# Four layers of token mixing on one core: 64-row products in alternate halves, compression products in column quarters, and a new order of the first transfers

## The reference, cut to what matters

```python
# compression (even layer): 15 windows of 32 tokens, 2 groups, window flattened to 4096
blk = (t[:, cmp_gather] + pe[:, None, :]).transpose(0, 1, 3, 2, 4).reshape(B, n_cmp, G, 32 * 128)
hid = silu(einsum('bcgf,fh->bcgh', blk, w1))        # w1: 4096 x 256
out = einsum('bcgh,hd->bcgd', hid, w2)              # once for keys, once for values
# retention, chunks of 128: contraction over 64
scores = einsum('bhtd,bhsd->bhts', qc, kc) * intra
# HGRN: a decay for each of the 64 channels between any two tokens of a chunk
scores = einsum('bhtd,bhsd,bhtsd->bhts', qc, kc, pair)
# RWKV
log_w = -DECAY * sigmoid(w0 + tanh(wd) @ w_up); a = sigmoid(a0 + ad @ a_up)   # 64 rows each
state = state * exp(lw) - (state @ kk) (a * kk) + v k ;  y = state @ r
```

## Time and profile before

| | us |
|---|---|
| median of 3 runs | 3870.77 (3852.96 to 3872.96) |
| the profiled execution | 3863.83 |
| its span | 3862.4 |
| PE busy | 3780.9 (98%), 19948 records |
| PE weight loads | 3190.6 (83%) |
| DVE busy | 2243.5 (58%) |
| ACT busy | 1793.4 (46%) |
| POOL busy | 113.0 (3%) |
| moved by DMA | 628.34 MB, mean 163 GB/s |
| mean granted clock of PE | 0.991 of full speed |

### The profile page before, as it was taken

The page is one execution under the profiler, slowest core; times in us unless marked ns, Lnnn a source line. Parts: engine busy times, 40 slices in busy tenths (PEclk is TensorE's granted clock), DMA queues, the critical chain, the costliest instruction groups (busy, mean ns, idle before and its releaser), DMA issues.

```text
span 3862.4 us, 49187 instructions
## 1 busy us (share of the span) xinstructions
PE 3780.9 (98%) x19948; PEld 3190.6 (83%) x19948; DVE 2243.5 (58%) x3532; ACT 1793.4 (46%) x2517; POOL 113.0 (3%) x61
## 2 busy tenths in 40 slices
PE   8999999999999999989999999999999999999998
PEld 7886778787898998778888888888987778888887
DVE  5665666676565746674455444566656764445444
ACT  6454545456554425454444444554335454444443
POOL 0000000000010000000000000010000000000000
PEclk9999999999999989999999999999999999999999
DMA  7655546563554315456666655544224456666654
GB/s 237 187 164 148 147 147 176 159 191 119 172 166 138 109 27 170 136 158 188 189 190 188 201 194 193 178 141 147 69 81 150 161 162 190 190 191 186 203 194 169
DMA packets 341426, 628.34 MB, mean 163 GB/s; under 512 B 21088, under 2 KB 63024, under 8 KB 340432
## 3 DMA queue, kind: packets, MB, share of 16 engines
q1 hardware_dynamic: 331920, 611.53, 52.5%
q10 hardware_dynamic: 9280, 13.69, 1.0%
HBM read 623.04 MB, written 2.10 MB: 162 GB/s over the span
## 4 chain that ended last, share of the span: by engine, by line
PE 92%; DVE 4%; ACT 2%; issue 1%; DMA 1%; POOL 0%; ACTq 0%; SPq 0%; DVEq 0%
PE bank L635 77%; PE bank L763 1%; DVE weights_low L529 1%; PE bank L1338 1%; PE bank L1435 1%; PE bank L2545 1%; PE bank L2559 1%; PE bank L2151 1%; PE bank L2558 1%; ACT weights_high L516 1%; PE bank L614 1%; PE bank L1418 1%; PE bank L1341 0%; PE bank L2512 0%; PE bank L1317 0%
## 5 line engine op out<-in xcount | busy, mean ns | idle before, releaser
L529 DVE TENSOR_TENSOR weights_low<-weights,weights_high 128x1024 fp32r<-128x1024 f32 (+3 forms) x1176 | 1392.4, 1194 | 994.2 <-ACT weights_high L516 983.4
L516 ACT ACTIVATE weights_high<-weights 128x1024 fp32r<-128x1024 f32 (+3 forms) x1176 | 1205.1, 1029 | 1308.6 <-PE bank L635 1250.8
L635 PE MATMUL bank<-weights_high,x_high 128*128 128x512 f32 (+3 forms) x2816 | 1111.4, 395 | 8.8 <-DVE weights_low L529 2.9
L635 PE MATMUL bank<-weights_low,x_high 128*128 128x512 f32 (+3 forms) x2816 | 1082.7, 384 | 0.0
L635 PE MATMUL bank<-weights_high,x_low 128*128 128x512 f32 (+3 forms) x2816 | 1081.4, 384 | 0.0
L635 PEld LDWEIGHTS bank<-weights_high,x_high 128*128 128x128 f32 x2816 | 532.3, 189 | 121.7 <-issue 15.1
L635 PEld LDWEIGHTS bank<-weights_low,x_high 128*128 128x128 f32 x2816 | 531.8, 189 | 101.5
L635 PEld LDWEIGHTS bank<-weights_high,x_low 128*128 128x128 f32 x2816 | 533.2, 189 | 92.8
L635 PE MATMUL bank<-x_high,weights_high 128*128 128x256 f32 x960 | 279.5, 291 | 9.5 <-DVE arena L664 4.8
L635 PE MATMUL bank<-weights_high,y_high 128*128 128x512 f32 (+1 forms) x672 | 266.7, 397 | 8.9 <-DVE weights_low L529 5.9
L635 PE MATMUL bank<-weights_high,ff_high 128*128 128x512 f32 x704 | 274.0, 389 | 0.0
(11 more groups left out here) (384 smaller groups left out, 3597.7 us busy)
## 6 DMA issues: line engine op xcount, KB each, us to landing
weights<-in_w_in_dram SPq DMA_DIRECT2D x208, 512.0 KB, 3.6
weights<-in_w_ffn_gate_dram SPq DMA_DIRECT2D x176, 512.0 KB, 3.7
weights<-in_w_ffn_up_dram SPq DMA_DIRECT2D x176, 512.0 KB, 3.7
weights<-in_w_ffn_down_dram SPq DMA_DIRECT2D x176, 512.0 KB, 3.6
weights<-in_w_out_dram SPq DMA_DIRECT2D x128, 512.0 KB, 3.7
weights<-in_even_w_in_dram SPq DMA_DIRECT2D x88, 512.0 KB, 3.6
weights<-in_odd_w_in_dram SPq DMA_DIRECT2D x80, 512.0 KB, 3.7
weights<-in_mem_w_kv_dram SPq DMA_DIRECT2D x32, 512.0 KB, 4.4
```

The source lines that it names most:

```text
L516: self.high_mark[g] = self.high_split.count(act.ran(nc.scalar.activation(high, raw, ACT.Copy)), act.clock)
L529: self.low_mark[g] = self.low_split.count(dve.ran(nc.vector.tensor_tensor(low, raw, high.bitcast(F32), ALU.subtract)), dve.clock)
L635: ins = pe.ran(nc.tensor.matmul(out, l, r, start=(u + c + x + y == 0), stop=(u == blk.n - 1 and c == UNIT - 1 and y == 1)))
```

## The change

Four edits. (1) In `retention`, `hgrn` (both places) and `rwkv` (three places), the products of two heads on opposite halves are issued in turn, into two banks, behind one wait for both banks; what follows on DVE and ACT stays as it was, head by head. PE's price of a 64-row product is halved in the planner when the one before lay on the other half. (2) A compression unit's four matmuls go to four quarters of the array's columns, 32 weights each, and so to partitions 0 to 127 of the bank; each quarter adds up a fourth of the sum. The bank is evacuated by a plain copy, and the transposes become products with a folded identity that add the quarters; ACT then applies Silu to the 60 columns. The planner's price of these units is the old one. (3) SP issues memory rows and weights in turn, two pieces and one unit, and a piece of x behind each of the units 8 to 15. (4) `first_turns` turns all memory rows with the splits between and the squares behind, and turns x only when block mem0.v is done.

```diff
@@ -206,7 +208,10 @@
             n = max(2 * n, 240)
         else:
             n = n + 32 if one.ins[0].dtype == F32R else max(4 * n + 24, 536)
-        self.clock += n / 2400
+        rows = one.tile_position[0] if one.ins[0].ap[0][1] <= HD2 else None
+        beside = rows is not None and self.rows not in (None, rows)
+        self.rows = rows
+        self.clock += n / 2400 / (2 if beside else 1)
         return ins
 
     def did(self, ins):
...
             self.plan()
-            for g in range(AHEAD):
+            for g in range(RAW):
                 self.load(g)
-            self.load_x()
-            for g in range(AHEAD, RAW):
-                self.load(g)
+                if g < 3:
+                    self.load_mem(g + 1)
             self.later = self.load_rest()
             for k in range(7):
                 next(self.later)
...
@@ -502,6 +506,14 @@
             dst = self.raw[i][:, :, 0:blk.width]
         self.sp.clock += 1.7
         self.load_mark[g] = self.loaded[i].count(self.nc.sync.dma_start(dst, blk.src[u]), self.sp.clock + 2.2)
+        if X_FROM <= g < X_FROM + 4 * T:
+            self.load_x((g - X_FROM) // T, (g - X_FROM) % T)
+
+    def split_to(self, g):
+
+        while self.split_next <= g:
+            self.split(self.split_next)
+            self.split_next += 1
 
     def split(self, g):
 
...
+            ins = pe.ran(nc.tensor.matmul(bank[l * QUARTER:(l + 1) * QUARTER, 0:CMP_HID], blk.AT[:, k * R2:k * R2 + QUARTER], wv[:, l, :],
+                                   start=(u == 0), stop=(u == blk.n - 1)))
         self.used_mark[g] = self.unit_used.count(ins, pe.clock + DRAIN)
         return self.used_mark[g]
 
...
+            self.sp.clock += 0.8
+            self.mem_loaded[nb].count(self.nc.sync.dma_start(self.mem[:, t, cut], self.A["mem"][0, t * P:(t + 1) * P, cut]), self.sp.clock + 2.5)
+
+    def load_x(self, nb, t):
+
+        cut = slice(nb * TILE, (nb + 1) * TILE)
+        self.sp.clock += 0.8
+        self.x_loaded[nb].count(self.nc.sync.dma_start(self.x[:, t, cut], self.A["x"][0, t * P:(t + 1) * P, cut]), self.sp.clock + 2.5)
 
     def load_rest(self):
 
...
@@ -979,7 +994,7 @@
 
         def evac(n, b, mark):
             act.wait_ge(mark)
-            m = act.did(nc.scalar.activation(self.hid[j][0:R2, :], self.ps[b][0:R2, 0:CMP_HID], ACT.Silu))
+            m = act.did(nc.scalar.activation(self.hid[j], self.ps[b][:, 0:CMP_HID], ACT.Copy))
             self.bank_free[b] = [m]
             return m
         return evac
...
-        yield
-        for nb in range(2, 4):
+        for nb in range(4):
             yield from turns(nb, self.hT_mem, *mem, self.mem_loaded[nb])
-            square(nb - 1, self.mem, self.mem_loaded[nb - 1])
+            if nb < AHEAD:
+                self.split_to(nb)
             yield
-        square(3, self.mem, self.mem_loaded[3])
+        for nb in range(4):
+            square(nb, self.mem, self.mem_loaded[nb])
+            yield
         self.rms_of(self.squares, self.scales["mem"])
         yield
+        yield from self.need("mem0.v")
         for nb in range(4):
             for _ in turns(nb, self.hT_even, self.x_chunk, self.col["norm0"], self.x_loaded[nb]):
                 yield _
...
         yield from self.need("e.kv0")
         self.ready(["e.kv0"], pe)
+        width = CMP_LEN * R2
+        for j in range(2):
+            dve.did(nc.vector.memset(self.blkT[j][:, width:width + 2], 0.0))
+        folded = dve.did(nc.vector.tensor_reduce(fold, self.c("ident").rearrange("p (g r) -> p r g", g=4), AX.X, ALU.add))
         for j in range(2):
             yield [*self.bank_free[6]]
             pe.wait_ge(*self.bank_free[6])
...
+            pe.wait_ge(folded, *self.bank_free[4])
             for c in range(2):
-                ins = pe.ran(nc.tensor.transpose(self.ps[4][:, c * R2:(c + 1) * R2], self.hid[j][0:R2, c * P:(c + 1) * P], self.c("ident")[0:R2, 0:R2]))
-            dve.wait_ge(pe.did(ins))
-            m = dve.did(nc.vector.tensor_copy(hidT[:, 0:2 * R2], self.ps[4][:, 0:2 * R2]))
+                ins = pe.ran(nc.tensor.matmul(self.ps[4][:, c * R2:(c + 1) * R2], self.hid[j][:, c * P:(c + 1) * P], fold[:, 0:R2], start=True, stop=True))
+            act.wait_ge(pe.did(ins))
+            m = act.did(nc.scalar.activation(hidT[:, 0:2 * R2], self.ps[4][:, 0:2 * R2], ACT.Silu))
             self.bank_free[4] = [m]
             yield
             yield [m, *self.bank_free[5]]
...
+            if h < H2 and h % 2 == 0:
+                at = h // 2 * S
+                both = [*self.bank_free[4], *self.bank_free[5]]
+                yield both
+                pe.wait_ge(*both)
+                for lo, cols in ((0, S), (P, P)):
+                    for e in range(2):
+                        half = slice(e * HD2, (e + 1) * HD2)
+                        ins = pe.ran(nc.tensor.matmul(self.ps[4 + e][:, 2 * lo:2 * lo + cols], kT[half, at + lo:at + lo + P],
+                                                      qT[half, at + lo:at + S], start=True, stop=True))
+                        if lo:
+                            scored[h + e] = pe.did(ins)
             if h < H2:
-                c, half, b = h // 2, slice(h % 2 * HD2, (h % 2 + 1) * HD2), 4 + h % 2
-                at = c * S
-                yield [*self.bank_free[b]]
-                pe.wait_ge(*self.bank_free[b])
-                pe.ran(nc.tensor.matmul(self.ps[b][:, 0:S], kT[half, at:at + P], qT[half, at:at + S], start=True, stop=True))
-                dve.wait_ge(pe.did(pe.ran(nc.tensor.matmul(self.ps[b][:, S:S + P], kT[half, at + P:at + S], qT[half, at + P:at + S],
-                                                    start=True, stop=True))))
+                b = 4 + h % 2
+                dve.wait_ge(scored[h])
                 if h >= 4:
                     dve.wait_ge(*weighed[h - 4][1:])
                 dve.did(nc.vector.tensor_tensor(sT[h % 4][:, 0:S], self.ps[b][:, 0:S], decay[:, h * S:(h + 1) * S], ALU.mult))
...
-                yield self.bank_free[b]
-                pe.wait_ge(*self.bank_free[b])
+            for pair in range(2):
+                both = [*self.bank_free[4 + 2 * pair], *self.bank_free[5 + 2 * pair]]
+                yield both
+                pe.wait_ge(*both)
                 for i in range(4):
-                    c, h = heads[4 * (g // 2) + g % 2 + 2 * (i // 2)]
-                    t = i % 2
-                    ins = pe.ran(nc.tensor.matmul(self.ps[b][:, i * P:(i + 1) * P], k3[h, c, t * P:(t + 1) * P], q3[h, c, t * P:(t + 1) * P],
-                                           start=True, stop=True))
-                multiplied[lev, g] = pe.did(ins)
+                    for e in range(2):
+                        g, t = 2 * pair + e, i % 2
+                        c, h = heads[4 * pair + e + 2 * (i // 2)]
+                        ins = pe.ran(nc.tensor.matmul(self.ps[4 + g][:, i * P:(i + 1) * P], k3[h, c, t * P:(t + 1) * P],
+                                                      q3[h, c, t * P:(t + 1) * P], start=True, stop=True))
+                        if i == 3:
+                            multiplied[lev, g] = pe.did(ins)
 
         def merge(lev, mask):
 
...
+        pe.wait_ge(*both)
+        crossed = []
+        for i in range(4):
+            for g in range(2):
                 c, h = heads[g + 2 * i]
                 ins = pe.ran(nc.tensor.matmul(self.ps[6 + g][:, i * P:(i + 1) * P], d3[h, c, 0:P], d3[h, c, P:S], start=True, stop=True))
-            act.wait_ge(pe.did(ins))
+                if i == 3:
+                    crossed.append(pe.did(ins))
+        for g in range(2):
+            act.wait_ge(crossed[g])
             m = act.did(nc.scalar.activation(cross[:, g * 512:(g + 1) * 512], self.ps[6 + g][:, :], ACT.Copy))
             self.bank_free[6 + g] = [m]
         yield from self.need(nm + "hgi", nm + "hgg")
...
+            for x in range(2):
+                for half in range(2):
+                    rows, c = slice(half * HD2, (half + 1) * HD2), 2 * pair + x
+                    ins = pe.ran(nc.tensor.matmul(self.ps[4 + 2 * pair + half][:, x * S:(x + 1) * S], lora[rows, c * P:(c + 1) * P], wa[rows, :],
+                                                  start=True, stop=True))
+                    if x:
+                        raised.append(pe.did(ins))
+            for half, (out, bias) in enumerate(((lw, "rwkv_w0_2"), (a, "rwkv_a0_2"))):
+                b, i = 4 + 2 * pair + half, 2 * pair + half
+                act.wait_ge(raised[half])
+                for x in range(2):
+                    c = 2 * pair + x
...
-                    n = 4 * grp + i
-                    t, c, e = units[n]
-                    b = 4 + i
-                    yield [*self.bank_free[b]]
-                    pe.wait_ge(*self.bank_free[b])
-                    pe.ran(nc.tensor.matmul(self.ps[b][:, 0:S].rearrange("p (k s) -> p k s", k=2), tile(a, c, t)[head(e), :], kr(c, t, e), start=True, stop=True))
```

(54 more changed lines are left out.)

61 lines of the change are left out of this document (24 added, 37 removed).

## The result

The changed kernel takes 3847.34 us (median of 17 runs, 3830.57 to 3860.82), the kernel before 3867.63 (17 runs). The ratio is 0.9949, 95% interval 0.9936 to 0.9962: 20 us faster (15 to 25), where 48 were forecast. The time lies inside the range of 3796 to 3852, near its slow end. The profiled execution took 3851.68, its span 3850.4, at a mean granted clock of 0.982, against 3863.83 at 0.991 before.

The account below looks back on a forecast made before the run. TensorE, holding 92% of the span, was taken as the bound. Halves 35, compression 12.5 and first transfers 4 give 51.5 us off 3863.8: 3812; clock cost makes 3817, half the median's 6.9 excess 3820 us; range 3796 to 3852.

Parts of the forecast that it names:

- The planner puts stream ahead of it as before, so I price it at 0: Each pair's wait for two free banks: stream chunks cover it, cost 0, up to 1.4 us a pair where they don't.
- All of it lies in PE's queue beside the stream of line 635, which fills every wait: The 35 us from pairing 64-row products: a shorter product makes the stream's next chunk earlier.
- the compression rival: Compression returns in full, as the planner or slack hides the softmax: 3812 us, up to 3806; chance 0.13.
- the clock in the compression stretch: Rival: the clock falls to 1.2 GHz during compression, adding up to 24 us: 3844 us; chance 0.08.
- Slower than before: Rival: waits on both banks stand open at 70 pairs, up to 1.4 us each: 3918 us at worst; chance 0.08.
- Retention, 5.5: Retention scores: pairing single heads and fewer changes between 64-row and 128-row work gain 5.5 us.
- RWKV, 8.4 + 2.3 + 1.7 = 12.4: RWKV pairs: scores gain 8.4 us, the products of line 2527 2.3, the two low-rank products 1.7.
- HGRN, 16 + 1.1: HGRN pairs: halves in turn gain 16 us at line 2151 and 1.1 us at line 2197.
- Compression, 12.5: Compression units shorten from 1.84 to 0.6 us; softmax waits limit the gain to 12.5 us, bounds 2 and 21.
- quarters don't overlap: Rival: in compression, one product's weights load only when the other is done; term drops to 2, 3830 us; chance 0.08.
- First transfers, 4.0: Kernel start: weights land earlier, near 8 us, so the stream starts 4.0 us earlier; bounds 2 and 5.
- Clock, 5: Cost against the gains: closer-packed products bring one or two more 7 us stretches at 1.2 GHz, 5 us.

Follow-up runs that it names:

- e6: The kernel before with only RWKV's products paired and the planner's halved charge for 64-row products: 3875.74 us, ratio 1.0038.
- e3: The whole change, but the planner charges 64-row products in full as before: 3826.75 us, ratio 0.9892 to the kernel before.
- e5: The kernel before with only RWKV's products paired and the planner's full charge kept: 3854.19 us, ratio 0.9978.
- e9: The kernel before, products unpaired, its planner charging 64-row products inside RWKV at half: 3922.46 us, ratio 1.0151.
- e10: The kernel before with all pairs and their two-bank waits, but products issued bank by bank, full charge: 3857.62 us, ratio 0.9975.
- e12: The whole change, but 64-row products charged in full inside RWKV only: 3816.20 us, ratio 0.9872 to the kernel before.
- e7: The kernel before with only HGRN's products paired, full charge: 3862.10 us, ratio 0.9993.
- e1: The kernel before with only the first transfers and the compression changed: 3850.6 us, ratio 0.9960.
- e11: The kernel before with all pairs issued in turn, full charge, first transfers and compression as before: 3845.45 us, ratio 0.9944.

## Why the prediction was wrong

**The step that failed** is "The planner puts stream ahead of it as before, so I price it at 0", and with it "All of it lies in PE's queue beside the stream of line 635, which fills every wait". The order was not as before. By the halved charge the planner saw a TensorE that was free earlier in RWKV, and put 120 more of the stream's records there. They filled nothing: TensorE had been busy for 231.97 of 232.5 us before, and the stretch grew by 29.8 us (in e6, with the same counts at a clock of 1.00 instead of 0.95, by 19.3). A mixing has a fixed number of chunks that don't need its own result, up to record 12192 here; spent in RWKV, they were missing in mLSTM's end and in retention, where the waits are then open and products behind them run at half clock for a while. e3 and the whole change differ by the charge alone: 0.9892 against 0.9949, some 22 us of the 28 that were missing. e5 and e6 repeat it with one part, e9 without any. The diff held the four lines of the charge in plain sight; the compression rival even named the planner's price, but only as to what a stale price does, never as to what a new one does.

How large it is in the trace: these are the whole mixings of layer 4, before, after and in e3, all work, columns as in the earlier trace rows.

```profile
2552.00:3114.00 562.00, 549.42 (x3454) 475.83 (x3454) 368.49 (x681) 244.44 (x367) 32.67 (x12) 1.00 0.41 125
2513.00:3102.00 589.00, 552.34 (x3455) 479.94 (x3454) 372.26 (x681) 247.01 (x369) 31.69 (x12) 0.94 0.39 119
2507.00:3072.00 565.00, 541.24 (x3458) 469.78 (x3456) 369.10 (x681) 246.00 (x369) 30.87 (x12) 0.98 0.41 125
```

The whole change is 24 us longer there than e3: TensorE is idle for 37 us instead of 24, and busy for 11 us more with the same products, at a clock of 0.94 instead of 0.98. The waits are 30.6 us in the stretch from 3000 to 3110, and three low-clock stretches behind 3005 (13.7, 30.7 and 6.8 us), at half speed, cost up to 25.6, partly at the same time. The timed runs say the same. At an equal mean clock of 0.987 three runs of e3 take 3830 us and one of the whole change 3838, and at 0.990 it is 3819 (one run) and 3831 (two). So of the 21 us between the medians 8 to 12 are waits and order, and the rest came with the clock, whose median is 0.983 in the whole change and 0.988 in e3. The four kernels with an emptied stream have median clocks of 0.982 to 0.986, the others 0.9865 to 0.990. That the open waits bring the clock down is argued from this, not shown by an experiment.

**The range.** That the time lies inside it is luck: its slow end was put there for the clock in the compression stretch and for waits at the pairs, and what came was neither.

**The rival that came true.** "Slower than before" had the open waits right as a mechanism and wrong in place: it looked for them at the pairs. In e10 the two-bank waits cost nothing. They were open only where the stream had run out (1.4 and 0.8 us at line 2041 in the list of waits), and they are a small part of it.

**Term by term.**
- *Retention, 5.5.* The task is 2.4 and 3.4 us shorter in e3, 5.8, and the same in e10: it came with the joint wait, bank by bank or in turn. The 3.8 and 4.8 of e12 have fewer stream records in them (25 for 31 in layer 4).
- *RWKV, 8.4 + 2.3 + 1.7 = 12.4.* e5 gives 8.5 us (3 to 14).
- *HGRN, 16 + 1.1.* The bursts fell as forecast: from first record to next, all of line 2177 takes 31.8 us for 50.6. e7 gives 2.7 us (-3 to 8). The stretches in e7 are 8.5 us shorter, and 13.1 in e12 (6.0 and 7.1), so the rest of e7's is the clock of RWKV behind it (0.92 for 1.00). At an equal mean clock of 0.987 three runs of e7 take 3862 us for some 3874 before, 12 us. "A shorter product makes the stream's next chunk earlier" fails where the stream, or HGRN's next products, are about to wait for DVE as well.
- *Compression, 12.5.* 18.0 less the head's 5.8 in e1: 12.2. Some 20 us went off the units and 12 off the kernel, as forecast. TensorE is idle for 5.9 us between 283 and 320 us, 0.7 before, which fits the softmax chain that was to set the pace; "full return" and "quarters don't overlap" both fall, at 0.57 us from a unit's first start to the next product, where 0.6 was forecast.
- *First transfers, 4.0.* 3.3 at the first record and 4.7 to 5.8 later.
- *Clock, 5.* Too small. Of the prediction's two marks of failure one came, a mean clock under 0.985 (0.982), and the other, idle time ahead of the pairs, did not: 1.5 us at line 2177 in the groups above.

In sum, 51.5 us were forecast ahead of the clock. e3 has 42 (35 to 48), with the order put right, and e12 50 (41 to 58), whose median of 3816 lies 4 us below the forecast of 3820, by an order that nobody had forecast. The products' own times were priced well, HGRN's return was put too high, and the order was not priced at all.

**What to carry to other kernels.** Where a planner writes the order at build time, a change of its costs is a change of the program: read what it moves before anything is priced, count the filler chunks left for each task, and look at the task that gets the fewest. A truer cost is no better order when the planner is greedy: the filler goes where it first fits, not where nothing else covers. And a saving in a queue counts only up to the next wait behind it.

## What the runs showed of the hardware

**The runs of one kernel spread with the granted clock.** Sorted by mean granted clock, the runs of before that were timed in the first round took 3875 us at 0.987 (3 runs), 3862 at 0.991 (2), 3852 at 0.994 (1), about 3.3 us for each 0.001; those of the changed kernel 3860 at 0.979 (2), 3848 at 0.983 (4), 3831 at 0.990 (2), about 2.6. At an equal clock of 0.987 it is 3874 before and 3838 after (one run). So the median gain of 20 us is some 36 us of work and waits less what the lower clock took. At this clock the parts add up: e1 gains 17 us (2 runs), e11 28 (1 run), and e3, which is both together, 44 (3 runs).

**The same records cost 5% more when the clock falls.** RWKV of layer 4, same order and same 1544 products: before and e1, all work.

```profile
2699.60:2932.10 232.50, 231.97 (x1544) 205.02 (x1544) 145.16 (x242) 91.51 (x135) 9.62 (x3) 1.00 0.32 94
```

```profile
2679.50:2923.40 243.90, 243.69 (x1544) 216.13 (x1544) 145.45 (x242) 91.77 (x136) 9.62 (x3) 0.94 0.31 89
```

The engine was listed as busy in both for all but 0.5 us of it, and 11.4 us went at a clock of 0.94 instead of 1.00. e7 has the same stretch at 0.92 and 248.1 us. Such falls came and went from trace to trace at the same work, which is why parts of 5 us need the median of many runs.

**Column quarters run beside each other.** From first start to the next product, eight records of 128x32 into quarters take 0.57 us where eight of 128x30 into one place took 1.84, 3.2 times as fast. The page "TensorE: Matmul & The Clock Gate" of the Trainium skill (Part 3, measured speedup) has 2.38 for three column tiles, and its rule on weight loads (What overlaps and what doesn't) would have them overlap only where the row group differs; the quarters are all of one row group, and the trace doesn't agree with it: the first four products start at 286.00 to 286.02, the next four at 286.24, and the weights of these are loaded at 286.03 to 286.05.
